# Ten of eleven down-projection units of a SwiGLU network as seven block products, and head 6's exponentials one place earlier

## What is computed

```python
D_FF = 2816
def swiglu(h, w_gate, w_up, w_down):
    return (jax.nn.silu(h @ w_gate) * (h @ w_up)) @ w_down

x = x + 0.5 * swiglu(rms_norm(x, norm[l]), w_gate[l], w_up[l], w_down[l])
```

```python
s = jnp.einsum('bhqd,bhkd->bhqk', q_blk, k).astype(jnp.float32) * scale
s = s + (c_blk[..., :, None] - c[:, :, None, :])
s = jnp.where(kpos[None, :] <= qpos[:, None], s, -jnp.inf)
p = jax.nn.softmax(s, axis=-1)
return jnp.einsum('bhqk,bhkd->bhqd', p.astype(v.dtype), v)
```

## Time and profile before

| what | us |
|---|---|
| median of 3 runs | 2299.2 (2299.05 to 2302.53) |
| the profiled execution | 2299.22 |
| its span | 2297.4 |
| TensorE busy | 2286.0 |
| VectorE busy | 1812.6 |
| ScalarE busy | 1381.5 |

### The profile page before, as it was taken

How to read it: one execution, slowest core, us unless ns; L and a number is a source line. 1 busy time by engine, 2 the same in 40 slices (tenths; PEclk the granted TensorE clock), 3 DMA queues, 4 the chain that set the end, 5 groups by cost and what they waited for, 6 DMA issues and landing times.

```text
span 2297.4 us, 33084 instructions
## 1 busy us (share of the span) xinstructions
PE 2286.0 (100%) x12395; PEld 1921.1 (84%) x12395; DVE 1812.6 (79%) x1974; ACT 1381.5 (60%) x1513; POOL 26.4 (1%) x32
## 2 busy tenths in 40 slices
PE   9999999999999999999999999999999999999999
PEld 7888889888888898888888888888888888888887
DVE  8887867788898877768889886577888888467987
ACT  6657466565566566556657555656565655564655
POOL 0000010000000000000000000000000000000000
PEclk9999999999999999999999999999999999999999
DMA  7666444566565554546556656546655665545653
GB/s 256 214 213 184 150 149 155 171 204 201 176 213 188 192 177 146 176 136 216 183 196 202 220 186 208 163 153 205 198 186 185 208 200 193 184 165 165 210 184 128
DMA packets 331063, 427.25 MB, mean 186 GB/s; under 512 B 17544, under 2 KB 296208, under 8 KB 330960
## 3 DMA queue, kind: packets, MB, share of 16 engines
q1 hardware_dynamic: 324832, 412.73, 55.0%
q10 hardware_dynamic: 4976, 9.52, 1.2%
q0 software_dynamic: 1152, 3.55, 0.5%
HBM read 424.69 MB, written 1.05 MB: 185 GB/s over the span
## 4 chain that ended last, share of the span: by engine, by line
PE 99%; DVE 1%; ACT 0%; issue 0%; ACTq 0%; DVEq 0%
PE ps L1371 15%; PE ps L1124 13%; PE ps L1126 13%; PE ps L1125 13%; PE ps L1236 13%; PE ps L1241 13%; PE ps L1237 13%; PE ps L1351 2%; PE ps L1137 1%; PE ps L1487 0%; PE ps L1556 0%; PE ps L1566 0%; DVE arena L2355 0%; PE ps L1718 0%; PE ps L1653 0%
## 5 line engine op out<-in xcount | busy, mean ns | idle before, releaser
L1859 DVE TENSOR_TENSOR wlo<-raw,whi 128x2048 fp32r<-128x2048 f32 x318 | 721.1, 2285 | 145.5 <-ACT whi L571 144.4
L571 ACT ACTIVATE whi<-raw 128x2048 fp32r<-128x2048 f32 x312 | 592.9, 1902 | 233.0 <-PE ps L1126 185.6
L1236 PE MATMUL ps<-whi,hT 128*128 128x512 f32 x1280 | 500.0, 391 | 0.0
L1237 PE MATMUL ps<-whi,hT 128*128 128x512 f32 x1280 | 498.4, 389 | 0.0
L1124 PE MATMUL ps<-whi,hT 128*128 128x512 f32 x856 | 342.8, 401 | 0.2
L1241 PE MATMUL ps<-wlo,hT 128*128 128x512 f32 x1280 | 342.4, 389 | 0.3 <-DVE wlo L1859 0.3
L1126 PE MATMUL ps<-whi,hT 128*128 128x512 f32 x856 | 334.2, 390 | 0.0
L1125 PE MATMUL ps<-wlo,hT 128*128 128x512 f32 x856 | 333.8, 390 | 0.0
L1236 PEld LDWEIGHTS ps<-whi,hT 128*128 128x128 f32 x1280 | 240.3, 188 | 53.1 <-ACT arena L688 2.8
L1241 PEld LDWEIGHTS ps<-wlo,hT 128*128 128x128 f32 x1280 | 239.6, 188 | 51.3 <-DVE wlo L1859 2.0
L1237 PEld LDWEIGHTS ps<-whi,hT 128*128 128x128 f32 x1280 | 240.3, 188 | 50.0
(11 more groups left out here) (336 smaller groups left out, 3049.9 us busy)
## 6 DMA issues: line engine op xcount, KB each, us to landing
raw<-in_w_ffn SPq DMA_DIRECT2D x264, 512.0 KB, 4.5
raw<-in_w_in SPq DMA_DIRECT2D x144, 512.0 KB, 4.8
raw<-in_ffn_w_down SPq DMA_DIRECT2D x88, 512.0 KB, 4.2
raw<-in_ffn_w_up SPq DMA_DIRECT2D x86, 512.0 KB, 4.1
raw<-in_ffn_w_gate SPq DMA_DIRECT2D x86, 512.0 KB, 5.4
raw<-in_w_out SPq DMA_DIRECT2D x32, 512.0 KB, 4.3
gain<-in_gains ACTq DMA_DIRECT2D x16, 512.0 KB
raw<-in_cross_wk SPq DMA_DIRECT2D x16, 512.0 KB, 4.1
```

The lines of the kernel that those rows point to most:

```text
L571: act.activation(whi[:, s, :, 0:cols], raw[:, s, :, 0:cols], ACT.Copy).then_inc(hi_ready, units)
L1236: pe.matmul(ps[:, bank, :], hT_hi[:, t, k0 + k, :], whi[:, s, k, :], start=first and k == 0, stop=False, skip_group_check=True)
L1237: pe.matmul(ps[:, bank, :], hT_lo[:, t, k0 + k, :], whi[:, s, k, :], start=False, stop=False, skip_group_check=True)
L1859: dve.tensor_tensor(wlo[:, s, :, 0:cols], raw[:, s, :, 0:cols], whi[:, s, :, 0:cols].bitcast(F32), ALU.subtract).then_inc(lo_ready, units)
```

## The change

BLOCKED becomes 10: down unit 9 is done as blocks too, and only unit 10 is plain. The banks of the seven block products are dealt out anew (the fourth number of each entry of BLOCKS), so that three of them are sums of their own piece and stay where they are: unit 10 accumulates on top of them. For the fourth piece the bank is copied away first (`first_kept`) and started afresh. Seven flush operations remain (FLUSHES was 11). The products of unit 9 are issued in the order of LAST_BLOCKS, the banks that must be read soonest first. Unit 10's weights are split in two halves on ScalarE and VectorE. Two flushes of piece 3 lie between the turns of the next operation's first pieces (`late_flush`). SP waits for unit 9's block sums before the next operation's loads. Apart from the FFN, head 6's exponentials come before head 5's copy on ScalarE.

```diff
-BLOCKED = FF_STEPS - 2
-BLOCKS = ((0, 0, 0, 0), (1, 0, 2, 1), (6, 0, 1, 2), (4, 1, 0, 3), (3, 1, 1, 5), (5, 2, 0, 6), (2, 2, 1, 7))
+BLOCKED = FF_STEPS - 1
+BLOCKS = ((0, 0, 0, 2), (1, 0, 2, 1), (6, 0, 1, 0), (4, 1, 0, 7), (3, 1, 1, 5), (5, 2, 0, 6), (2, 2, 1, 3))
...
+LAST_BLOCKS = tuple(3 * m + part for m in (0, 5, 3, 4, 1, 2, 6) for part in range(3))
+FLUSHES = 7
@@ SP
-                with sp.Fori(0, BLOCKED) as c:
+                with sp.Fori(0, BLOCKED - 1) as c:
...
                 down(off + FFN_UNITS - 1, 0, FF_STEPS - 1)
+                sp.wait_ge(block_summed, 3 * BLOCKED * (ffn_no(b, l, e) + 1))
@@ ACT
+                act.activation(whi[:, s, 0:2, :], raw[:, s, 0:2, :], ACT.Copy).then_inc(half_hi, 1)
+                act.activation(whi[:, s, 2:4, :], raw[:, s, 2:4, :], ACT.Copy).then_inc(hi_ready, 1)
+                second_silu(last)
                 act.wait_ge(block_used, 2 * BLOCKED * (f + 1) - 1)
...
+                act.activation(first_two[:, 0, :], ps[:, BLOCKS[0][3], :], ACT.Copy).then_inc(first_kept, 1)
...
                 fox_pT(4)
+                fox_exp(6)
                 fox_pT(5)
-                fox_exp(6)
                 fox_exp(7)
@@ PE
+                def last_blocks(items):
...
+                        if n in (5, 11):
+                            mm.then_inc(block_used, 1)
...
+                        own = at == 1
+                        if own:
+                            pe.wait_ge(first_kept, f + 1)
...
+                pe.wait_ge(block_lo_ready, 3 * BLOCKED * (f + 1))
+                last_blocks(range(0, 8))
                 turn_act(last, at=((0, 1), (2, 3)))
-                down(last - 1, order[2:4], False)
+                last_blocks(range(8, 21)).then_inc(unit_done, 1)
                 pe.wait_ge(act_lo, FF_STEPS * (f + 1))
                 wait_weights(b, l, off + FFN_UNITS - 1)
-                pe.wait_ge(flushed, FLUSHES * (f + 1))
@@ DVE
+                bank_product(last)
                 dve.wait_ge(first_kept, f + 1)
-                dve.tensor_tensor(first_two[:, 1, :], first_two[:, 0, :], ps[:, TR, :], ALU.add).then_inc(both_kept, 1)
...
+                dve.tensor_tensor(both, kept, ps[:, bank[5], :], ALU.add).then_inc(both_kept, 1)
+                flush(2, kept, ALU.add)
                 dve.wait_ge(act_hi, FF_STEPS * (f + 1))
...
+                dve.wait_ge(block_used, 2 * BLOCKED * (f + 1))
+                dve.wait_ge(both_kept, f + 1)
+                dve.wait_ge(flushed, FLUSHES * f + 1)
+                dve.tensor_tensor(kept, ps[:, bank[3], :], both, ALU.subtract).then_inc(flushed, 1)
+                flush(0, kept, ALU.add, 2)
+                flush(1, kept, ALU.add)
+                flush(1, ps[:, bank[4], :], ALU.add, 4)
...
+                dve.wait_ge(flushed, FLUSHES * f + 5)
...
                 split_lo(b, l, off + FFN_UNITS)
...
+                for i in range(PIECES):
+                    if i == PIECES - 2:
+                        turn_out(T + 1, (0,))
+                        late_flush(True)
+                        turn_out(T + 1, (1,))
+                        late_flush(False)
+                    if i == PIECES - 1:
+                        dve.wait_ge(flushed, FLUSHES * (f + 1))
+                    add(b, l, j, i, off + FFN_UNITS - 1, 1.0)
+                    gained(A, n + 1, i, (b, l, e) == (0, DEPTH - 1, 1))
```

119 lines of the change are left out of this document (56 added, 63 removed).

## The result

The changed kernel takes 2311.77 us (median of 6 runs, 2311.28 to 2312.15) against 2299.7 for the kernel before (6 runs): a ratio of 1.005, 95% interval 1.0039 to 1.006. It is slower, as forecast (2312.8). The profiled execution took 2311.79 us, its span is 2310.0 against 2297.4, and the +12.6 (12.57) between the spans are what follows.

What follows compares the result with a forecast made beforehand. The prediction took TensorE to bound the kernel, everything else hidden behind it by margins. FFNs +16.6 us (matmul saving included) less 3.0 at head 6 gave +13.6 on 2299.2: 2312.8 us, range 2306 to 2318.

Steps and rivals of the forecast that it cites:

- tail: End of an FFN, seven of eight alike: waits of 2.7 us against 0.68 saved, a loss of 2.0 us each.
- The stretch laid out: First FFN's end: VectorE's chain of sums after unit 9's products, first gain product ending at 188.5 instead of 187.43.
- Wait 1: TensorE waits for VectorE's gain product before transposing the next input's first piece: 1.3 us.
- wait 2: TensorE waits for the gain product before the third piece's transposes: 0.8 us.
- wait 3: TensorE waits for VectorE's low part of the third piece before the unit after it: 0.6 us.
- Extras: Joint gain or scaling on VectorE delaying the last transposes, and small work ahead of wait 3: 1.9 us over three FFNs.
- The last FFN: No next weights there; half a microsecond arrives at the end instead of 0.68 saved: +0.5 us.
- Head 6: TensorE's 1.77 us wait at L1556, twice, shrinks or goes with exponentials earlier: 3.0 us gained in all (2.4 to 3.6).
- (a): Rival: VectorE's sums at the FFN ends stay hidden, 5.5 + 3.0 us gained, 2290.7; chance 0.08.
- (c): Rival: head 6 gains nothing because GpSimd's instructions hold the scalings to their end, +16.6, 2315.8; chance 0.12.
- (b): Rival: VectorE's dependent links do not cost 0.18 us more; each tail loses 1.5, FFNs +10.8, 2307; chance 0.13.
- (d): Rival: only part of the waits at FFN ends appear, 2 to 8 us slower, 2301 to 2306; chance 0.09.

Runs made afterwards that it cites:

- the kernel with all orders changed: Changed kernel with another order of TensorE's matmuls in the first two units behind an FFN and VectorE's end-of-FFN instructions spread out: 2300.79 us.

## Why the prediction was right, step by step

**Bound by TensorE, with margins.** Right: the tails' 15.0 us are margins overdrawn, and the loss follows VectorE's list, not the matmuls. That no row of the waits had TensorE waiting on weights was not quite so: there are two such rows in the kernel before, 0.3 us each, once each, and they are the same after.

**Matmuls removed, 0.68 us in each FFN.** Exact: -0.68 in the last FFN, and -0.68, -0.68 and -0.70 at the first piece of the three kernels that have no wait there.

**The stretch laid out.** The first gain product was to end at 188.5; it ended at 188.61 in a trace that runs 0.28 late from the start of the program, so 188.33. Wait 1 is 1.18 (said: 1.3), wait 2 0.74 (0.8), wait 3 0.52 (0.6). What was mis-sized is the link between dependent instructions: 0.12 us more than an independent start instead of 0.18 (182.16 to 182.88), except between first add and gain product, where it is 0.18 (187.14 to 187.92) as in the row that it was taken from the earlier trace rows. The traces say where to look: 13 times in the changed kernel the first gain product of a group of pieces starts 0.79 to 0.80 after its add, and all others start 0.71 to 0.73 after theirs; the other traces show the same two groups. The 13 are the products that also wait for the gain to be loaded (gain_loaded). In the last FFN that wait stands ahead of the add, and the product starts 0.73 after it. So the second wait is the likely cause; no run takes it away. A tail came to 1.92 where 2.0 was said; its waits alone, less 0.68, make 1.76, and the rest is 0.05 us more at each group of transposes or matmuls that had to wait. The sum has a slip: 7 x 2.0 is 14.0, not 14.2.

**The hole.** The prediction has the low part of the second turned piece end at 192.25; it ended at 192.23 on the same clock. It did not say that 0.54 us of idle time lay ahead of it, so its account of the loss ("VectorE is a chain") was incomplete: 0.5 of the 1.92 us was a matter of one line's place.

**Extras.** 1.6 us over three FFNs where 1.9 was said: 0.71 in the one with the joint gain, 0.40 in the one with the scaling, and 0.49. The waits before the last transposes came only in the two FFNs named. The joint gain itself cost only 0.13 (0.62 where the first tail has 0.49 at the first piece); the rest of the 0.71, and the 0.49, is wait 3, which was 1.04 in two FFNs, since small work stands ahead of the third piece's low part there.

**The last FFN.** +0.5 said, -0.68 + 1.19 = +0.51 measured. **Loads: nothing**, right for TensorE: no wait of it on hi parts came into any tail. But a margin shrank: at 206.17 ScalarE waits 1.76 us for a load, which it did not in the kernel before, and the kernel with all orders changed overdrew this one. FFNs together +15.5 against +16.6.

**Head 6.** -3.0 said (2.4 to 3.6), -3.5 to -3.6 measured, at the edge: in both layers one scaling was held by one GpSimd instruction and the other passed at its boundary, and the whole wait went. The 3.0 was a middle taken between two outcomes that the one example left open. In the kernel with this edit alone they were free at 321.81, where the prediction had 321.5 to 321.6 for this case.

**Rivals.** (a), the sums stay hidden, and (c), no gain at head 6, are out. (b), waiting on oneself is cheap, was right by a third: 0.06 of 0.18. Its total was added up wrongly: seven tails at 1.5 us with the same extras make +12.9, not +10.8, and 2309.1, not 2307. (d) is out; all three waits came in all seven tails.

**The total.** By spans the sum is +12.6 against +13.6: the FFNs 1.1 less than said, head 6 0.3 more gained (with the pause counted against it), and 0.3 at the start that is not the edit's. The waits were right for the reasons given, and their sizes within 0.12 us; that the total is within 1.0 us of 2312.8 is in part luck, since the 0.28 of the start and the pause of 0.29, neither of them the edit's, bring it nearer.

## What to carry to other kernels

Where one engine is full and another works through a list beside it, an edit that moves work into the list's last stretch costs what it makes that list longer, waits for round trips included, as long as the full engine needs the results in the same order; lay the list out before counting matmuls saved. Here no order and no help from GpSimd made the FFN edit pay: the best of them took 2298.85 us, and the kernel with head 6's order alone 2296.05. The cheapest repair is the order: work that nobody waits for belongs into the round trip, and an independent instruction between two dependent ones. Before an instruction is moved later, look at everything that its end releases, the loads too; before work is given to GpSimd, look at which of VectorE's instructions beside it read both inputs from SBUF, since the two engines then wait for each other.

## What the runs showed of the hardware that I had not expected

- GpSimd and VectorE: a scaling of VectorE (one input, 128 and 256 columns) is held until GpSimd's instruction ends (2.21 us for two that take 0.55), and so is a sum or product with two SBUF inputs (3.31 for 2.29, 1.00 for 0.69). One with an input in the accumulator memory is not touched (0.68).
- It goes both ways. Where VectorE's instruction had started first, GpSimd's was held: 1.68 us beside 0.51 us of a sum, 3.35 beside 2.19 us of a low part, for an instruction that takes 1.28 or 1.29 otherwise. With 0.05 us between the starts it went either way at head 6: the first scaling was held in the changed kernel (2.55 us) and not in the kernel with head 6's order alone (0.29).
- In the profile of the kernel with the FFN edit alone, TensorE's wait of 1.77 us at head 6 in the first layer was followed by eight steps of 0.43 us in place of 0.23, with a granted clock of 0.72 on the mean of the six microseconds from 326 (the column behind GpSimd's share below): the lower of the clock's two levels (1.2 and 2.4 GHz) for eight matmuls. This adds 1.6 us to that profile's span (2316.79 us in a series with a median of 2315.56). In the six microseconds before 326 the granted clock was 1.00, with TensorE busy for 4.81 of them. After the same wait in the kernel before, and in the second layer of this one, it stayed full.

```profile
326.00:332.00 6.00, 5.42 (x20) 4.37 (x21) 3.34 (x5) 1.41 (x3) 0.37 (x1) 0.72 0.25 72
```
